# Fifth gate column block in fp32r triples, and one exponential per head with its accumulated sum, in a hybrid decoder layer

## The reference

```python
proj = jnp.einsum('btd,dc->btc', h, w_in)
q, k, v, z, gates = _split(proj, (ATTN_WIDTH, KV_WIDTH, KV_WIDTH, SHIFT_WIDTH, 2 * D_MODEL))
...
m = jnp.maximum(jnp.max(scores, axis=-1, keepdims=True), sink)
p = jnp.exp(scores - m)
probs = p / (jnp.sum(p, axis=-1, keepdims=True) + jnp.exp(sink - m))
out = jnp.einsum('bnhgqk,bnkhd->bnqhgd', probs, vw)
...
merged = jax.nn.sigmoid(ga) * (attn.astype(h.dtype) @ w_branch_a) \
    + jax.nn.sigmoid(gb) * (y.astype(h.dtype) @ w_branch_b)
```

## Time and profile before

| what | value |
|---|---|
| time, median of 3 runs | 1711.48 us (1711.03 to 1711.93) |
| the profiled execution: time, span | 1710.47 us, 1708.7 us |
| TensorE busy | 1423.5 us (83%) |
| VectorE busy | 735.6 us (43%) |
| ScalarE busy | 434.7 us (25%) |
| GpSimd busy | 49.3 us (3%) |
| chain that ended last, by engine | TensorE 51%, DMA 40%, VectorE 5%, ScalarE 2% |

### The profile page before, as it was taken

The page is one execution under the profiler, slowest core; times in us unless marked ns, Lnnn a source line. Parts: engine busy times, 40 slices in busy tenths (PEclk is TensorE's granted clock), DMA queues, the critical chain, the costliest instruction groups (busy, mean ns, idle before and its releaser), DMA issues.

```text
span 1708.7 us, 26529 instructions
## 1 busy us (share of the span) xinstructions
PE 1423.5 (83%) x11614; PEld 873.9 (51%) x11614; DVE 735.6 (43%) x1101; ACT 434.7 (25%) x601; POOL 49.3 (3%) x40
## 2 busy tenths in 40 slices
PE   7999999988899999999787686776776767767766
PEld 6888888757777788886232141232322322322322
DVE  6666554578476766553322232223231322322232
ACT  5444444345353434444100000000000000000002
POOL 3000000001103010000000000000000000000000
PEclk9999999999999999999888888888888888888888
DMA  9645456231231493858999999999999999999996
GB/s 349 222 175 185 150 205 225 75 111 52 65 94 43 176 340 123 335 208 350 423 433 432 429 433 433 432 432 431 432 432 432 433 431 430 433 433 431 432 427 291
DMA packets 80539, 529.31 MB, mean 310 GB/s; under 512 B 7840, under 2 KB 10154, under 8 KB 65866
## 3 DMA queue, kind: packets, MB, share of 16 engines
q1 hardware_dynamic: 75584, 514.50, 73.9%
q0 software_dynamic: 2224, 9.35, 1.5%
q10 hardware_dynamic: 2650, 4.26, 0.7%
HBM read 521.80 MB, written 6.29 MB: 309 GB/s over the span
## 4 chain that ended last, share of the span: by engine, by line
PE 51%; DMA 40%; DVE 5%; ACT 2%; issue 2%; DVEq 0%; SPq 0%; ACTq 0%
DMA ring<-in_expert_w_up 14%; DMA ring<-in_expert_w_gate 12%; PE ps L1084 10%; DMA ring<-in_expert_w_down 8%; PE ps L669 7%; PE ps L1193 7%; PE ps L730 5%; DMA arena<-in_expert_w_up 4%; PE ps L1329 3%; PE ps L670 3%; PE ps L769 3%; DMA arena<-in_expert_w_gate 2%; PE ps L747 1%; PE ps L632 1%; PE ps L1283 1%
## 5 line engine op out<-in xcount | busy, mean ns | idle before, releaser
L2291 DVE TENSOR_TENSOR arena<-arena,ps 128x512 f32<-128x512 f32 x248 | 154.0, 682 | 403.0 <-PE ps L1181 402.1
L1193 PE MATMUL ps<-ring,arena 128*32 128x512 f32 x1024 | 156.7, 763 | 93.1 <-DMA ring<-in_expert_w_gate 56.0
L1193 PE MATMUL ps<-arena 128*32 128x512 f32 x1018 | 149.0, 732 | 81.4 <-DMA arena<-in_expert_w_up 50.3
L669 PE MATMUL ps<-h_both,w_hi 128*128 128x512 f32 x544 | 194.6, 402 | 1.9 <-DVE w_lo L1857 1.9
L670 PE MATMUL ps<-h_both,w_lo 128*128 128x256 f32 x544 | 153.7, 283 | 0.0
L1193 PEld LDWEIGHTS ps<-ring,arena 128*32 128x32 f32 x1024 | 37.5, 134 | 207.5 <-issue 97.6
L1193 PEld LDWEIGHTS ps<-arena 128*32 128x32 f32 x1018 | 37.3, 130 | 181.5 <-issue 119.3
L669 PEld LDWEIGHTS ps<-h_both,w_hi 128*128 128x128 f32 x544 | 103.3, 190 | 28.3 <-DVE w_lo L1857 2.5
L1915 DVE TENSOR_TENSOR w_lo<-ring,w_hi 128x1024 fp32r<-128x1024 f32 (+1 forms) x62 | 74.4, 1199 | 82.7 <-ACT w_hi L1497 82.4
L1987 DVE TENSOR_TENSOR v_lo<-ring,v_hi 128x1024 fp32r<-128x1024 f32 x64 | 78.3, 1224 | 69.1 <-ACT v_hi L1527 68.7
L1716 ACT ACTIVATE arena<-ps 128x512 f32<-128x512 f32 x32 | 33.7, 1052 | 280.6 <-PE ps L1193 272.7
(11 more groups left out here) (341 smaller groups left out, 2125.6 us busy)
## 6 DMA issues: line engine op xcount, KB each, us to landing
arena<-in_expert_w_gate SPq DMA_DIRECT2D x15, 4096.0 KB, 32.7
ring<-in_expert_w_gate SPq DMA_DIRECT2D x15, 4096.0 KB, 32.8
arena<-in_expert_w_up SPq DMA_DIRECT2D x15, 4096.0 KB, 32.3
arena<-in_expert_w_down SPq DMA_DIRECT2D x15, 4096.0 KB, 33.4
ring<-in_w_in SPq DMA_DIRECT2D x28, 2048.0 KB, 7.7
ring<-in_expert_w_up SPq DMA_DIRECT2D x14, 4096.0 KB, 33.4
ring<-in_expert_w_down SPq DMA_DIRECT2D x14, 4096.0 KB, 34.3
ring<-in_w_out SPq DMA_DIRECT2D x8, 2048.0 KB, 8.2
```

The costliest lines, as they stand in the source:

```text
L669: mm(out, hi[:, 128 * n:128 * n + 128], both(k), start=start and n == 0, stop=False)
L1193: last = mm(ps[32 * c:32 * c + 32, bank, :], XS[:, k, 32 * j:32 * j + 32], w[c], start=i == 0, stop=i == 3, tile_position=(0, 32 * c))
L2291: last = v.tensor_tensor(xs, xs, ps[:, banks[nb], :], ALU.add)
```

## The change

Block 4 of the gates is computed like blocks 5 to 7. `gate_mm` is gone; `fill_mm`, `f_hi` and `f_lo` count pieces from y = -16, and `fill_mm` stands at the same places with the same counts (8, 1, 1, 5, 1, 1, 15). The pieces y = -16 to -9 are made ahead of the attention, the others between its units. Waits that counted `chunk_used` for block 4 now count `w_used`, or `ND` in the place of `NF`.

In the softmax, `shifted` no longer subtracts the maximum from the scores; it writes its negative into `nmax`. `exponentials` takes each head by itself, with that head's column of `nmax` as bias, and with the sum of its row written to `esum` (`accum_out`). `normed` no longer sums. Here is the core of the diff; the hunks that only exchange `NF` for `ND` in waits for later loads are left out:

```diff
         UF = (8 - GD - 1) * KT
-        F0 = UZ + UX
+        UY = KT
+        F0 = UZ + UX + UY
+        ND = NG + 2 * GD
         UPG = 3 * GE
         EW = 2 * SLOT
 
@@ -466,7 +470,7 @@
             for g in range(UF // 4):
                 c = 2 * GD + 2 + g // 2
                 s, o = slot_of(NG + c), 4 * (g % 2)
-                sp.wait_ge(*((S("chunk_used"), NF - 1 + g // 2) if g < 4 else (S("w_used"), 4 + F0 + 4 * (g - 3))))
+                sp.wait_ge(S("w_used"), 4 + F0 + (8 * (g // 2 - 1) if g < 4 else 4 * (g - 3)))
                 sp.dma_start(ring[:, s, 512 * o:512 * o + 2048].rearrange("p (k n) -> p k n", k=4),
                              cols(GA0 + 512 * (c // 2), c % 2, 512)[:, o:o + 4, :]).then_inc(f_sem(g), 16)
             wa = a["w_branch_a"][0].rearrange("(k p) n -> p k n", p=P)
@@ -731,28 +735,7 @@
                                       start=n == 0 and i == 0 and p == 0, stop=n == 7 and i == 1 and p == 2)
                 last.then_inc(S("w_used"), 1)
 
-            gate_part = [0]
-
-            def gate_mm(count):
-
-
-                for m in range(gate_part[0], gate_part[0] + count):
-                    k, t = divmod(m, TT)
-                    n = NG + 2 * GD + k // 8
-                    if k == 0:
-
-                        pe.wait_ge(S("gate_out"), 2 * GD - 1 + t)
-                    if t == 0 and k % 8 == 0:
-                        full(n)
-                    last = mm(ps[:, 6 + t, :], hT[:, k, 128 * t:128 * t + 128], slot(n)[:, k % 8, :],
-                              start=k == 0, stop=k == KT - 1)
-                    if t and k % 8 == 7:
-                        last.then_inc(S("chunk_used"), 1)
-                    elif k == KT - 1:
-                        last.then_inc(S("gate_ps"), 1)
-                gate_part[0] += count
-
-            fill_part = [0]
+            fill_part = [-TT * UY]
 
             def fill_mm(count):
 
@@ -813,19 +796,19 @@
             pe.wait_ge(S("gate_out"), 4)
             scores(0)
             scores(1)
-            gate_mm(8)
+            fill_mm(8)
             scores(2)
-            gate_mm(1)
+            fill_mm(1)
             turned(0)
-            gate_mm(1)
+            fill_mm(1)
             values(0)
-            gate_mm(5)
+            fill_mm(5)
             scores(3)
-            gate_mm(1)
+            fill_mm(1)
             turned(1)
-            gate_mm(1)
+            fill_mm(1)
             values(1)
-            gate_mm(15)
+            fill_mm(15)
             turned(2)
             fill_mm(FILL_A)
             values(2)
@@ -1467,6 +1450,22 @@
                 act.wait_ge(S("zs_done"), 5 + 24 + t + 1)
                 f(lz[0:m, t, :], zs[0:m, t, :], ACT.Copy, scale=omm[0:m, t:t + 1]).then_inc(S("za_done"), 1)
 
+            f_at = [-UY]
+
+            def f_hi(upto):
+
+
+                for y in range(f_at[0], max(upto, f_at[0])):
+                    if y < 0 and y % 8 == 0:
+                        n = NF + y // 8
+                        act.wait_ge(S(f"slot_full{n % RING}"), 16 * (n // RING + 1))
+                    elif y >= 0 and y % 4 == 0:
+                        act.wait_ge(f_sem(y // 4), f_landed(y // 4))
+                    if y >= 8 - UY:
+                        act.wait_ge(S("w_used"), 4 + F0 + y - 7)
+                    f(f_pieces(y)[0], f_src(y), ACT.Copy).then_inc(S("w_hi"), 1)
+                f_at[0] = max(upto, f_at[0])
+
             gate_tile = [0]
 
@@ -1477,8 +1476,7 @@
                 if b < GD:
                     act.wait_ge(S("w_used"), 4 + UZ + UQ + UL + 8 * b + 8)
                 else:
-                    act.wait_ge(*((S("gate_ps"), b + 1 - GD) if t == 0 else (S("chunk_used"), NF) if b == GD else
-                                  (S("w_used"), 4 + F0 + KT * (b - GD))))
+                    act.wait_ge(*((S("gate_ps"), b + 1 - GD) if t == 0 else (S("w_used"), 4 + F0 + KT * (b - GD))))
                 if q >= 2:
 
                     act.wait_ge(S(f"gate_stored{t}"), 16 * b)
@@ -1511,6 +1509,8 @@
                         act.wait_ge(S("z_done"), 4 + 27)
                     gate_out()
                     gate_out()
+                if x == UX:
+                    f_hi(8 - UY)
             act.wait_ge(S("z_done"), 4 + 27)
             f(lz[0:64, 0, :], lz[0:64, 0, :], ACT.Tanh).then_inc(S("lora_done"), 1)
             f(lz[:, 1, :], lz[:, 1, :], ACT.Sigmoid).then_inc(S("lora_done"), 1)
@@ -1529,7 +1529,10 @@
             def exponentials(u):
 
                 act.wait_ge(S("sm_done"), u + 1)
-                f(probs_of(u), probs_of(u), ACT.Exp).then_inc(S("ex_done"), 1)
+                for h in range(8):
+                    last = f(probs_of(u)[:, h, :], probs_of(u)[:, h, :], ACT.Exp, bias=nmax2[:, u % 2, h:h + 1],
+                             accum_out=esum2[:, u % 2, h:h + 1])
+                last.then_inc(S("ex_done"), 1)
                 f(aes2[:, u % 2, :], aes2[:, u % 2, :], ACT.Exp).then_inc(S("ex_done"), 1)
 
@@ -1547,26 +1550,15 @@
 
             exponentials(0)
             exponentials(1)
+            f_hi(-4)
             turned_out(0)
             values_out(0)
+            f_hi(-1)
             exponentials(2)
             turned_out(1)
             values_out(1)
+            f_hi(0)
             exponentials(3)
-            f_at = [0]
-
-            def f_hi(upto):
-
-
-                for y in range(f_at[0], max(upto, f_at[0])):
-                    if y % 4 == 0:
-                        act.wait_ge(f_sem(y // 4), f_landed(y // 4))
-                    if y >= 8:
-                        act.wait_ge(S("w_used"), 4 + F0 + y - 7)
-                    f(f_pieces(y)[0], f_src(y), ACT.Copy).then_inc(S("w_hi"), 1)
-                f_at[0] = max(upto, f_at[0])
-
-            act.wait_ge(S("chunk_used"), NF)
             f_hi(1)
             gate_out()
             gate_out()
@@ -1929,6 +1921,20 @@
 
             dve.wait_ge(S("const_in"), 16)
             dve.wait_ge(S("small_in"), 16 * 9)
+
+            f_at = [-UY]
+
+            def f_lo(upto):
+
+
+                for y in range(f_at[0], max(upto, f_at[0])):
+                    hi, lo = f_pieces(y)
+                    dve.wait_ge(S("w_hi"), F0 + y + 1)
+                    v.tensor_tensor(lo, f_src(y), hi.bitcast(F32), ALU.subtract).then_inc(S("w_lo"), 1)
+                f_at[0] = max(upto, f_at[0])
+
+            f_lo(8 - UY)
+
             def shifted(u):
 
                 n, hg = divmod(u, 2)
@@ -1944,7 +1950,7 @@
                 step(v.tensor_reduce(amax[:, :], probs, AX.X, ALU.max))
                 step(v.tensor_tensor(amax[:, :], amax[:, :], sink[:, 8 * hg:8 * hg + 8], ALU.max))
                 step(v.tensor_tensor(aes, sink[:, 8 * hg:8 * hg + 8], amax[:, :], ALU.subtract))
-                v.tensor_tensor(probs, probs, rep(amax[:, :], w), ALU.subtract).then_inc(S("sm_done"), 1)
+                v.tensor_scalar(nmax2[:, u % 2, :], amax[:, :], -1.0, None, ALU.mult).then_inc(S("sm_done"), 1)
 
             def normed(u):
 
@@ -1953,8 +1959,7 @@
                 dve.wait_ge(S("ex_done"), 2 * u + 2)
                 if u:
                     dve.wait_ge(S("pr_done"), u)
-                step(v.tensor_reduce(asum[:, :], probs, AX.X, ALU.add))
-                step(v.tensor_tensor(asum[:, :], asum[:, :], aes, ALU.add))
+                step(v.tensor_tensor(asum[:, :], esum2[:, u % 2, :], aes, ALU.add))
                 step(v.reciprocal(asum[:, :], asum[:, :]))
                 v.tensor_tensor(probs, probs, rep(asum[:, :], w), ALU.mult).then_inc(S("pr_done"), 1)
 
@@ -1963,20 +1968,12 @@
             normed(0)
             shifted(2)
             normed(1)
+            f_lo(-1)
             shifted(3)
+            f_lo(0)
             normed(2)
+            f_lo(1)
             normed(3)
-            f_at = [0]
-
-            def f_lo(upto):
-
-
-                for y in range(f_at[0], max(upto, f_at[0])):
-                    hi, lo = f_pieces(y)
-                    dve.wait_ge(S("w_hi"), F0 + y + 1)
-                    v.tensor_tensor(lo, f_src(y), hi.bitcast(F32), ALU.subtract).then_inc(S("w_lo"), 1)
-                f_at[0] = max(upto, f_at[0])
-
             f_lo(4)
             dve.wait_ge(S("pv_ps"), 4)
 
```

More of the change, by code:

```diff
@@ L159, in hybrid_layer @@
         amax = sb("amax", [P, 8])
+        nmax2 = sb("nmax", [P, 2, 8])
+        esum2 = sb("esum", [P, 2, 8])
         aes2 = sb("aes", [P, 2, 8])
@@ L476, in _ @@
                     sp.wait_ge(S("yc_done"), HALVES)
-                sp.wait_ge(*((S("w_used"), 4 + F0 + UF - 8 + 8 * min(c, 1)) if c < 4 else (S("chunk_used"), NF + c - 3)))
+                sp.wait_ge(*((S("w_used"), 4 + F0 + UF - 8 + 8 * min(c, 1)) if c < 4 else (S("chunk_used"), ND + c - 3)))
                 sp.dma_start(ring[:, c % RING, :].rearrange("p (k n) -> p k n", k=8),
@@ L490, in _ @@
             for c in range(8):
-                sp.wait_ge(S("chunk_used"), NF + 5 + c if c < 2 else NF + 8 + c - 1)
+                sp.wait_ge(S("chunk_used"), ND + 5 + c if c < 2 else ND + 8 + c - 1)
```

(6 more changed lines are left out.)

## The result

The changed kernel took 1702.99 us (median of 5, 1700.56 to 1705.61) where the kernel before took 1711.48 (median of 5, 1708.75 to 1712.13) beside it. The ratio is 0.995, 95% interval 0.9936 to 0.9964. It was timed once more beside other kernels: 1704.04 against 1710.59, ratio 0.9956 (0.9941 to 0.9972). By these medians the change wins 6.5 to 8.5 us; the forecast was 6.8.

A forecast was written before the change was run, and what follows sets the result against it. In attention the last fp32 gate matmul, then ScalarE's table load and sigmoids, bound the end. Gates ending 4.4 us earlier and that load leaving give 6.8: profiled 1710.47 to 1703.7, median 1704.7; 8-in-10 range 1702.2 to 1708.8.

The forecast's parts named there:

- A triple is 0.70 us: TensorE's gate fills: three fp32r matmuls take 0.70 us, replacing an fp32 matmul of 0.87; 2.6 us won after values(1).
- Exponentials 0.48 and 0.37 a head: ScalarE's softmax: with bias and accumulator, a head takes 0.48 us for 256 columns, 0.37 for 128.
- The copies queue ahead of values(0) and of exponentials(2): ScalarE's f_hi copies: four delay turned_out(0), so TensorE waits about 2 us; three more put exponentials(2) at 348.2.
- VectorE ends 4 us ahead: End of attention: normed(2) ends at 360.4, TensorE's fills at 364.8, so VectorE has 4 us in hand.
- The table load leaves the chain: ScalarE before turned_out(2): copy and table load, formerly 369.4 to 371.34, are over before the last gate matmul ends.
- 6.8 us in the stage: End of the attention stage: turned_out(2) starts at 366.75 instead of 373.58, 6.8 us earlier.
- The tail moves as a block: Expert-weight loads from about 800 us: whatever is won before them starts them that much earlier.
- the forecast's own range: Whole time 1702.8 to 1707.1 us, from the bounds of the exponentials and the triple's 0.68; chance 0.62.
- The clock rival: TensorE's clock falls or a dip moves, 1.7 us each: one or two more, 1706.4 to 1708.1, chance 0.15; one fewer, 0.07.
- The win is swallowed: Rival: gate-weight loads bind or the expert stream does not start earlier; 1709 to 1711.5 us, chance 0.1.
- Slower, if a head costs 0.3 more: Rival on ScalarE's exponentials: 0.3 us more a head loses the win; at 0.5 more, 1716 us; chance 0.06.
- 24d less the slack: ScalarE's delay before the last fills if each head in exponentials(0) to (2) costs d more; slack 0.3 us.

The follow-up runs named there:

- e3: Changed kernel with two groups of f_hi copies one place later on ScalarE, behind turned_out(0) and exponentials(2); 1704.17 us, 0.9953 of the kernel before.
- e7: e1 with unused matmuls of constants filling TensorE's two long waits, ahead of scores(2) and turned(2); 1711.31 us, 1.0009 of the kernel before.
- e10: The changed kernel itself, unaltered, timed and profiled once more; 1704.04 us, 0.9956 of the kernel before.
- e1: Changed kernel with only the gates as triples, the softmax as in the kernel before; 1713.30 us, 1.0016 of the kernel before.
- e6: Changed kernel with every head's exponential split into two over half the keys each; 1713.58 us, 1.0017 of the kernel before.
- e5: e3 with only four of VectorE's eight subtractions ahead of shifted(3), the other four behind it; 1705.64 us, 0.9968 of the kernel before.
- e4: Changed kernel without accumulated sums in the exponentials, the row sum back on VectorE; 1700.74 us, 0.9945 of the kernel before.

## Why the prediction was right

- **A triple is 0.70 us.** Right: 45 matmuls in 10.59 us are 0.706 a triple, and the last run took 10.6 where 10.5 was forecast and 13.1 was before.
- **Exponentials 0.48 and 0.37 a head.** Right, a trifle low: the piece of eight heads of 256 keys is 3.94 us, 0.49 each; 0.385 of 128 keys. The read of the accumulator took 0.19 and the next head started 0.10 behind the start of the read (347.77 and 347.87 above), where the earlier trace rows had 0.09.
- **The copies queue ahead of values(0) and of exponentials(2).** Right: 1.86 us of wait for about 2 forecast; exponentials(2) started at 347.4, 3.2 us after shifted(2) had ended, for 2.9 forecast. e3 moved them and the waits went.
- **VectorE ends 4 us ahead.** Right: 5.3 us. **The table load leaves the chain.** Right, by 2.0 us.
- **6.8 us in the stage.** 6.69, and again 6.69 in the second profile. The two parts hold too: the last gate matmul was forecast 4.4 us earlier and turned(2) came 4.26 earlier; the rest, 2.4, measured 2.43.
- **The tail moves as a block.** Right within 1 us: the expert stage began 8.6 us earlier, and the span ended 7.6 us earlier.
- **The rest of the 8.5 us is not the change's.** The two profiled executions are 7.6 us apart in their spans: 0.95 before the stage, where the two programs do the same, 6.69 in it, 0.9 from there to the experts, less 1.0 in the experts. The 0.9 may be the dip of the kernel before, nine matmuls in 3.84 us behind a wait of 2.14, where the changed kernel took 2.29 for them at 425.83. No run tests it, and the stretch from the nine filling matmuls behind the stage to the experts differs by 2.4 us between the profiles (391.4 us in the changed kernel, 393.8 in e7). What is left of the 8.5 is that this execution of the kernel before was 1.0 us below its median. So the second timing, 6.5 us, is the better match for 6.7, and that the first came near the lower end of the forecast's own range (1702.8) is partly the chance of which executions were timed.
- **The clock rival** was sized wrong. I priced a dip at 1.7 us and tied it to a place, so that the change would move it or not. A fall comes and goes between executions at one place, as the changed kernel and e10 show, and one can cost 4.7. In the attention itself it stayed away: the changed kernel's granted clock was 1.00 over 341 to 345 us, across the wait of 1.86 us, where e1's was 0.69 and 0.61 behind waits of 2.56 and 3.29 and e6's 0.50 and 0.66 around waits of 4.69 and 2.80. For the two places of e1, e7 ties the fall to the wait. How long a wait has to be for that is not shown: the spell came behind waits of 0.5 to 0.9 us. So the size of this rival was wrong: a spell of 4.7 us is more than the two dips (3.4) that it allowed for.
- **The win is swallowed:** no sign of it, in any of the profiles.
- **Slower, if a head costs 0.3 more:** the break-even was right as far as it went. e6 added 0.28 a head and lost 10.6 us in the stage, of which 6.4 by ScalarE's queue, as the sum 24d less the slack has it, and 4.2 by the clock, which the rival left out.

## What to carry to other kernels

When two engines are both nearly full in a stage, test the two reliefs apart and together: here each alone gave 1.4 us or nothing, both gave 6.7. Ask also what an engine's last instruction holds back elsewhere: 2.4 of the 6.7 us came from a copy and a table load that no longer waited for the last gate matmul. Work moved to the engine with idle time should be placed behind what others wait for; seven copies, in two groups one place too early, cost the stage 1.3 us. And an accumulated sum that relieved an engine with slack at the price of the one on the chain was a loss here: without it the stage was 0.9 us shorter.

## What the runs showed of the hardware that was not expected

TensorE's granted clock fell to half (0.50 over 381 to 385 us in e5) while the engine was busy throughout, behind a stretch of transposes, small matmuls and waits of 0.5 to 0.9 us, and stayed low for some 10 us. Three of the twelve profiles show it right behind the attention, e5, e6 and e10: 25.70 to 25.74 us from turned_out(2) to the nine filling matmuls, where the other nine profiles took 20.96 to 21.09. What brings it on stays open.

At 4.7 us it is the largest difference that I found between two executions of one kernel at one place, but not the only one. The gate run's start differs by up to 4.3 us between profiles (237.79 in e4, 242.11 in the kernel before; 3.3 between the changed kernel's two), and the stretch from the experts' first piece to the end by 3.1 (921.8 us in the kernel before, 925.0 in e4). The kernel before spread over 1705 to 1718 us in 23 executions. Against that, differences of 1 us are better read from a stage's length, which for the changed kernel was 124.78 twice, than from medians.
